# Even key pages of a paged decoder step: one product and one sum on VectorE in the place of eight fused products

## The reference, cut to what matters

```python
k_past = cache_k[l][page_table].reshape(dec_b, -1, SB_HEADS, SB_HEAD_DIM)
...
z = jnp.einsum('bhqd,bhkd->bhqk', q.astype(jnp.float32), k.astype(jnp.float32)) * (SB_HEAD_DIM ** -0.5)
```

## Time and profile before

| | |
|---|---|
| median of 3 runs | 1495.51 us (1494.76 to 1495.96) |
| profiled execution, its own time | 1496.05 us |
| its span in the profile | 1494.3 us |
| PE busy | 1428.4 us, 96% |
| DVE busy | 921.6 us, 62% |
| ACT busy | 665.5 us, 45% |
| even pages (L1312), all their product records | 256 records, 56.8 us |
| odd pages on DVE (L1306) | 32 records, 39.0 us |

### The profile page before, as it was taken

How to read it: one execution, slowest core, us unless ns; L and a number is a source line. 1 busy time by engine, 2 the same in 40 slices (tenths; PEclk the granted TensorE clock), 3 DMA queues, 4 the chain that set the end, 5 groups by cost and what they waited for, 6 DMA issues and landing times.

```text
span 1494.3 us, 29193 instructions
## 1 busy us (share of the span) xinstructions
PE 1428.4 (96%) x11238; PEld 1273.0 (85%) x11238; DVE 921.6 (62%) x1519; ACT 665.5 (45%) x1303; POOL 103.8 (7%) x200
## 2 busy tenths in 40 slices
PE   6779999998899999998999999999999999999997
PEld 2247787887667777796899999999999999999997
DVE  2243588995777666368756766567665675446444
ACT  1023477777656454345543434434344343334333
POOL 0000311113322210000000000000000000200000
PEclk9979999999899999999999999999999999999999
DMA  9999999999999979985755565555655555855552
GB/s 370 422 343 364 390 391 405 374 352 391 396 370 343 340 255 356 409 307 225 250 182 183 170 193 173 181 182 170 191 174 181 182 170 192 231 181 181 181 178 95
DMA packets 139330, 396.82 MB, mean 266 GB/s; under 512 B 13162, under 2 KB 17681, under 8 KB 126433
## 3 DMA queue, kind: packets, MB, share of 16 engines
q1 hardware_dynamic: 118018, 319.66, 61.3%
q0 software_dynamic: 21232, 76.10, 13.4%
HBM read 382.28 MB, written 11.34 MB: 263 GB/s over the span
## 4 chain that ended last, share of the span: by engine, by line
PE 83%; DMA 11%; DVE 2%; ACT 2%; issue 1%; POOLq 0%; SPq 0%; POOL 0%; DVEq 0%; ACTq 0%
PE ps L1981 24%; PE ps L1982 24%; PE ps L1983 24%; DMA ada_s<-in_w_ada 5%; PE ps L1915 4%; DMA v_page<-in_cache_v 3%; PE ps L2113 2%; DMA ada_r<-in_w_ada 1%; PE ps L2039 1%; DMA raw<-in_w_ffn_gate 1%; DMA k_page<-in_cache_k 1%; ACT k_page L803 1%; DMA k_page<-in_cache_v 1%; ACT w_hi L715 0%; PE ps L2141 0%
## 5 line engine op out<-in xcount | busy, mean ns | idle before, releaser
L1981 PE MATMUL ps<-h_hi,w_hi 128*128 128x264 f32 x2304 | 667.8, 290 | 11.0 <-DVE h_lo L1249 3.6
L1982 PE MATMUL ps<-h_lo,w_hi 128*128 128x264 f32 x2304 | 659.2, 286 | 0.0
L1983 PE MATMUL ps<-h_hi,w_lo 128*128 128x264 f32 x2304 | 658.6, 286 | 0.0
L1981 PEld LDWEIGHTS ps<-h_hi,w_hi 128*128 128x128 f32 x2304 | 438.9, 190 | 55.8 <-issue 34.9
L1806 DVE TENSOR_TENSOR w_lo<-raw,w_hi 128x1024 fp32r<-128x1024 f32 x254 | 307.2, 1214 | 273.1 <-ACT w_hi L1047 271.7
L1047 ACT ACTIVATE w_hi<-raw 128x1024 fp32r<-128x1024 f32 x264 | 278.5, 1059 | 408.2 <-PE ps L1983 384.4
L1982 PEld LDWEIGHTS ps<-h_lo,w_hi 128*128 128x128 f32 x2304 | 438.2, 190 | 0.5
L1983 PEld LDWEIGHTS ps<-h_hi,w_lo 128*128 128x128 f32 x2304 | 436.9, 190 | 0.0
L1261 DVE TENSOR_TENSOR w_lo<-raw,w_hi 128x1024 fp32r<-128x1024 f32 x138 | 168.7, 1223 | 145.9 <-ACT w_hi L715 145.5
L715 ACT ACTIVATE w_hi<-raw 128x1024 fp32r<-128x1024 f32 x128 | 135.1, 1056 | 172.5 <-PE ps L1983 155.1
L1982 PE MATMUL ps<-act_lo,w_hi 128*128 (+1 forms) x704 | 200.4, 285 | 0.0
(11 more groups left out here) (362 smaller groups left out, 1213.8 us busy)
## 6 DMA issues: line engine op xcount, KB each, us to landing
ada_r<-in_w_ada SPq DMA_DIRECT2D x64, 1024.0 KB, 9.1
raw<-in_w_in SPq DMA_DIRECT2D x96, 512.0 KB, 8.3
raw<-in_w_ffn_gate SPq DMA_DIRECT2D x88, 512.0 KB, 3.5
raw<-in_w_ffn_up SPq DMA_DIRECT2D x88, 512.0 KB, 4.4
raw<-in_w_ffn_down SPq DMA_DIRECT2D x88, 512.0 KB, 4.6
ada_s<-in_w_ada SPq DMA_DIRECT2D x32, 1024.0 KB, 13.7
k_page<-in_cache_k POOLq DMA_DIRECT2D x64, 512.0 KB, 8.0
v_page<-in_cache_v POOLq DMA_DIRECT2D x38, 512.0 KB, 8.4
```

What stands on the lines that cost most here:

```text
L1981: mm(out, w_hi, xh, start=first, stop=False)
L1982: mm(out, w_hi, xl, start=False, stop=False)
L1983: return mm(out, w_lo, xh, start=False, stop=last)
```

## The change

For an even page DVE now does one product over the whole page, 128 x 1024, in place, as for an odd page. It waits for it through `link`, and then one reduction adds up the 128 values of each of the 8 heads and writes the 8 sums to the same place in `z_dec`. The reduction raises `k_even`. Odd pages, and all other engines, have the code that they had.

```diff
                     pg = n % PAGES
-                    for h in range(H):
-                        hs = slice(h * DH, (h + 1) * DH)
-                        ins = v.scalar_tensor_tensor(kp[:, hs], kp[:, hs], 1.0, QBC[:, b % 2, hs], ALU.mult, ALU.mult,
-                                                     accum_out=ZD[:, b, pg * H + h:pg * H + h + 1])
-                    ins.then_inc(k_even, 1)
+                    link(v.tensor_tensor(kp[:, :], kp[:, :], QBC[:, b % 2, :], ALU.mult))
+                    v.tensor_reduce(ZD[:, b, pg * H:pg * H + H], kp[:, :].rearrange("p (h d) -> p h d", h=H), op=ALU.add,
+                                    axis=AX.X).then_inc(k_even, 1)
```

## The result

The changed kernel takes 1504.77 us (median of 7 runs, 1501.55 to 1505.47) against 1495.96 us before (7 runs, 1493.62 to 1499.02). The ratio is 1.006, with an interval of 1.005 to 1.007: slower by 8.8 us, where 5.5 was forecast. Differences of times in this document are differences of medians, each against the kernel before in the same group of runs. The profiled execution took 1503.72 us, its span 1502.1 us, 7.8 longer than before.

A forecast was written before the change was run, and what follows sets the result against it. PE, DVE and the DMAs were taken as nearly full together where the pages run. Terms of 2.8, 3.2 and -0.5 gave +5.5 us, forecast 1501.0 us; range 1497.5 to 1504.5, 8 times in 10 1496.5 to 1509.5.

The forecast's parts named there:

- The price of a page: On DVE, an even page takes 2.39 us (1.25 to the sum, 1.14 for it), 0.69 more than now.
- The way to PE: Weight residues made ahead hide several us of DVE's lag; two other ways pass it to PE.
- the two named waits: PE's 1.60 us before unit 32 and 0.60 us at the last tree product, where DVE's lag reaches it.
- 189 to 240 us: Ten even pages add 6.9 us on DVE against 4.6 of idle; 2.8 taken to reach PE, bounds 2.3 and 6.9.
- 260 to 324: Seven even pages add 4.8 us against 1.6 of DVE idle; 3.2 reach PE in full at the tree product.
- rival 2: DVE's idle time absorbs nothing, copies and loads shifting in a closed ring; 15.9 us reach PE, 1511.4; chance 0.12.
- 240 to 260: Two even pages add 1.4 us against 3.4 of DVE idle: nothing more; at most 2.0 us won back.
- 345 to 425: Nine even pages add 6.2 us against 25.8 of DVE idle; -0.5 taken, between +1 and -6.
- All hidden: Slack on DVE and PE hides the added work: +0 to +2 us, 1496.5; chance 0.15.
- All of it passes: DVE's idle time absorbs nothing before 345 us; 23 pages pass 15.9 us to PE, 1511.4; chance 0.12.
- A sum as slow as a running sum: On DVE the sum makes each even page +3.02 us; about +55 us, 1550; chance 0.04.
- Faster: From 189 to 260 us later key page loads let ada and weight loads land sooner; 1 to 3 us won, 1493.5; chance 0.07.

The follow-up runs named there:

- half_sum: The changed kernel with the sum of an even page over only 64 of each head's 128 products; 1494.41 us, 1.0001 of the kernel before.
- evac_first: The changed kernel with three of ACT's four projection evacuations at the end of slot 31 ahead of its page sums; 1503.85 us, 1.0055 of the kernel before.
- tree_first: The changed kernel with DVE's last tree product ahead of the two key pages of slot 50; 1504.70 us, 1.0063 of the kernel before.
- both_first: The changed kernel with evacuation ahead of page sums in slot 31 and tree product ahead of pages in slot 50; 1503.48 us, 1.0056 of the kernel before.
- pad_small: The kernel before, but after an even page's fused products DVE waits and writes zeros over 64 used columns; 1494.15 us, 0.9995.
- pad_large: The kernel before, but after an even page's fused products DVE waits and writes zeros over 1024 used columns; 1512.26 us, 1.0120.
- before_both_first: The kernel before (fused products) with evacuation ahead of page sums in slot 31 and tree product ahead of pages in slot 50; 1496.28 us, 1.0010.

## Why the prediction was right in kind and short by a third

The measured 1504.77 us lies 0.3 us above the forecast's own range (1497.5 to 1504.5) and inside that for 8 times in 10 (1496.5 to 1509.5).

**The price of a page**: right, 2.39 us, with the sum at 1.14 from start to start. The Trainium skill, "VectorE: DVE Perf Modes", section on the perf-mode tier table, has tensor_reduce at one element per cycle only; the trace agrees, 1.22 us for 1024 elements and 0.69 for 512. The advice on the hot path, which the prediction took for that section's too, stands under "Rules for kernel authors" of the same page, as "Consider restructuring". That page's errata section has (N+151)/0.96 ns for an fp32 tensor_tensor add; an estimate from it makes the new form 0.12 us a page dearer than the old. The formula gives the listed 1.22 and 0.69 of the reduction well; what it has wrong here is the eight short products, which start 0.21 us apart and not 0.29. What a page dearer by 0.12 us would have done, half_sum shows at 0.16: nothing. So this one term decided between no change and a loss.

**The way to PE**: right. The residues hid the lag, the two named waits passed it on, and the last nine pages are free. What the prediction left out is that these waits are only the first that PE meets (evac_first, tree_first, both_first).

**How much DVE's idle time absorbs, and the clock**: this is where the forecast fell short. It had a lag of 2.8 us from "189 to 240 us" and 3.2 from "260 to 324", 6.0 together; at unit 52 it is 9.8. DVE's own lag, less unit 20's -0.5, parts the 3.8 missing. Behind the ten pages of the first stage it is 4.6 (a residue, L1261, starts at 239.64 before and at 243.74 now): 1.8 more than forecast. At the last tree factor it is 8.3 (321.99, 329.85): it grew by 3.7, 0.5 more than forecast. The rest, 1.5, is PE at the lower clock behind that wait, for which the sum had no term at all. PE's +4.7 at unit 34 (5.2 above unit 20) holds some of the first slow stretch too, so it isn't DVE's lag alone.

In the first stage 4.1 us of the 6.9 added were taken as absorbed, and 2.3 were. DVE's waits in that stretch, before and then after:

```profile
DVE w_lo L1261 <- ACT w_hi L715: 4.8, 3, 3.1
DVE k_page L1312 <- DMA k_page<-in_cache_k: 2.2, 3, 1.2
DVE k_page L1306 <- DMA k_page<-in_cache_k: 0.3, 1, 0.3
```

```profile
DVE w_lo L1261 <- ACT w_hi L715: 3.1, 1, 3.1
DVE k_page L1310 <- DMA k_page<-in_cache_k: 2.8, 2, 2.4
```

Both are of the stretch from 189 to 236 us. The wait of 3.1 us ends at 188 us, ahead of the first page. Of the rest only the waits for weight copies went (1.7 us). Those for pages grew from 2.5 to 2.8, for a page's load hangs on DVE itself. In the changed kernel, POOL's loads and the late page:

```profile
217.91 0.53 POOL L573 DMA_DIRECT2D k_page<-in_cache_k  x1 [4.75 <-DVE z_dec L1311]
219.07 0.53 POOL L573 DMA_DIRECT2D k_page<-in_cache_k  x1 [0.63 <-issue]
...
228.49 1.23 DVE L1310 TENSOR_TENSOR k_page<-k_page,q_bcast 128x1024 f32<-128x1024 f32 x1 [2.35 <-DMA k_page<-in_cache_k]
```

and the same two loads and page before:

```profile
216.03 0.53 POOL L573 DMA_DIRECT2D k_page<-in_cache_k  x1 [3.51 <-DVE k_page L1312]
217.20 0.53 POOL L573 DMA_DIRECT2D k_page<-in_cache_k  x1 [0.63 <-issue]
...
225.99 0.29 DVE L1312 SCALAR_TENSOR_TENSOR k_page<-k_page,q_bcast 128x128 f32<-128x128 f32 x1 [0.82 <-DMA k_page<-in_cache_k]
```

The first load is held by DVE's own even page and the second stands right behind it; both are issued 1.9 us later, and the page is used 2.5 us later. (Which load brings which page is my count of the order; the rows don't name it.) Idle time of this kind moves with the lag, as far as these rows show it; no run breaks the ring. It is the ring of rival 2, which the prediction gave 0.12 and refused because of the waits for copies: it holds for the part of the idle time that waits for pages. The weight of that part stood in the earlier trace rows, 2.9 us, and the sum didn't use it.

In "240 to 260" no more lag was to come, and DVE has 4.7 us at the first tree products (249.54, 253.73). In "345 to 425" the forecast had -0.5 and -0.7 is seen from unit 52 to 72, but the difference swings between +7.5 and +10.7 on the way: the size is luck.

**The sum**: 5.2 to unit 34, 0.3 to unit 42, 4.3 at unit 52, -0.7 to unit 72, and -0.5 from unit 20's offset, is 8.6, where the prediction had 2.8 + 3.2 - 0.5. The span grew by 7.8. Of the changes behind unit 72 the fall from +9.3 to +7.9 between units 127 and 132 stands against the same trace of before in half_sum (1.3), pad_small (1.6) and pad_large (1.5) too, whatever a page costs there, so it is hardly the new pages' work; the rest of them stays open. The last key page starts 10.7 us later (419.10, 429.81) and not some 5, and "from 460 us on no further difference" holds to 1 or 2 us.

**Rivals.** "All hidden" is what pages dearer by 0.16 to 0.19 us do. "All of it passes" fell as a whole, true in the part named. A sum as slow as a running sum fell by its 1.22 us. "Faster" has nothing for it: PE's wait for `ada_r` fell from 1.7 to 0.6 us, and the time still rose.

## What to carry to other kernels

Price a short fused instruction by starts, not by its listed duration: here eight that accumulate take 1.70 us, and one long product and a separate pass over all 1024 values 2.39. In this kernel the idle time of a nearly full engine absorbed added work where it waited for another engine's copies, and not where it waited for buffers that it frees itself; take those out before the rest is counted as slack. Beyond the slack three quarters of the added time and more came out, and reordering the place where PE first meets it moved the wait and won nothing that was measured. Where a longer wait is forecast for TensorE, ask what the clock behind it costs, and give it a term.

## What the runs showed of the hardware

- A fused product with accumulation over 128 fp32 elements starts every 0.21 us in a row, its accumulator read (0.08) hidden. A reduction costs as much per fp32 element as the two-source product: 1.22 us for 1024.
- A fill of 64 columns that waits for its predecessor costs 0.19 us with the link; one of 1024 columns, listed at 0.91, costs 1.19.
- PE stood 1.60 us and ran on at 2.4 GHz (matmuls 0.12 us apart); it stood 5.16 us and ran one whole unit at a granted 0.50, 1.2 GHz, 0.22 apart, 5.41 us instead of 2.99. With PE kept at work through that wait, it was 1.00. In before_both_first it stood 2.20 us, until 239.13, and ran at a granted 0.50 from 240 to 242 us.
